# A two-layer decoder step on one core: the decay/alpha low-rank layer run on raw rows, token-shift differences on GpSimd

## The reference, cut to what matters

```python
h = _rmsnorm(x, p["norm_mix_g"][i])                  # the third norm of the program
h_prev = jnp.concatenate([shift0[:, None, :], h[:, :-1]], axis=1)
xx = h_prev - h
mixed = h[None] + xx[None] * mu[:, None, None, :]
r, k, v = jnp.einsum("sbtd,sde->sbte", mixed[:3], w_rkv)
xv, xw, xa, xg = mixed[2], mixed[3], mixed[4], mixed[5]
w_log = -jax.nn.softplus(-(w0 + jnp.tanh(xw @ w1) @ w2)) - 0.5
alpha = jax.nn.sigmoid(a0 + (xa @ a1) @ a2)
g = jax.nn.sigmoid(xg @ g1) @ g2
```

## Time and profile before

| | before |
|---|---|
| runs, us | 1533.9 (1532.29 to 1537.23) |
| the profiled execution, us | 1532.43 |
| its span, first to last instruction | 1530.0 |
| mean granted TensorE clock | 0.993 |
| busy share PE / DVE / ACT / POOL | 97% / 71% / 56% / 9% |

### The profile page before, as it was taken

The page is one execution under the profiler, slowest core; times in us unless marked ns, Lnnn a source line. Parts: engine busy times, 40 slices in busy tenths (PEclk is TensorE's granted clock), DMA queues, the critical chain, the costliest instruction groups (busy, mean ns, idle before and its releaser), DMA issues.

```text
span 1530.0 us, 26537 instructions
## 1 busy us (share of the span) xinstructions
PE 1489.8 (97%) x11503; PEld 1215.8 (79%) x11503; DVE 1085.8 (71%) x1038; ACT 857.6 (56%) x838; POOL 134.5 (9%) x170
## 2 busy tenths in 40 slices
PE   7999999999999988999999999999999999999997
PEld 7998999999889778986667677776777777777674
DVE  4687455554468664222498898888888888888897
ACT  5444444433364423233367777777777777777775
POOL 0066100000100030133001000000000000000020
PEclk9999999999999999999999999999999999999999
DMA  8643575545345020055599999999999999999992
GB/s 250 191 145 83 150 230 164 164 129 153 83 141 188 4 58 4 21 125 175 204 317 383 382 380 366 383 374 381 386 373 384 364 388 372 366 387 367 381 388 97
DMA packets 250269, 378.05 MB, mean 247 GB/s; under 512 B 28169, under 2 KB 142073, under 8 KB 249858
## 3 DMA queue, kind: packets, MB, share of 16 engines
q1 hardware_dynamic: 247874, 370.04, 69.6%
q0 software_dynamic: 2064, 6.18, 1.2%
q10 hardware_dynamic: 208, 0.07, 0.0%
HBM read 368.47 MB, written 7.78 MB: 246 GB/s over the span
## 4 chain that ended last, share of the span: by engine, by line
PE 94%; DVE 3%; issue 1%; ACT 1%; DMA 0%; ACTq 0%; DVEq 0%
PE bank L2562 46%; PE bank L1927 27%; PE bank L2050 3%; PE bank L2224 1%; PE bank L2209 1%; DVE wL L1612 1%; PE bank L2470 1%; PE bank L2495 1%; PE bank L2571 1%; PE bank L1980 1%; PE bank L2409 1%; PE bank L2543 0%; PE bank L2417 0%; PE bank L2271 0%; DMA vecrows<-b_w 0%
## 5 line engine op out<-in xcount | busy, mean ns | idle before, releaser
L1612 DVE TENSOR_TENSOR wL<-ering,wH 128x2048 fp32r<-128x2048 f32 x264 | 603.4, 2289 | 89.4 <-ACT wH L1105 88.0
L1105 ACT ACTIVATE wH<-ering 128x2048 fp32r<-128x2048 f32 x264 | 506.0, 1917 | 147.5 <-PE bank L2562 147.3
L2562 PE MATMUL bank<-wH,xgH 128*96 128x512 f32 (+1 forms) x768 | 290.1, 378 | 2.0 <-DVE wL L1612 1.6
L2562 PE MATMUL bank<-wH,xgL 128*96 128x512 f32 (+1 forms) x768 | 287.6, 374 | 0.0
L2562 PE MATMUL bank<-wL,xgH 128*96 128x512 f32 (+1 forms) x768 | 287.3, 374 | 0.0
L2562 PEld LDWEIGHTS bank<-wH,xgH 128*96 128x96 f32 x768 | 124.4, 162 | 46.1 <-issue 2.1
L2562 PEld LDWEIGHTS bank<-wH,xgL 128*96 128x96 f32 x768 | 124.3, 162 | 44.3 <-issue 0.3
L2562 PEld LDWEIGHTS bank<-wL,xgH 128*96 128x96 f32 x768 | 124.5, 162 | 42.1
L2562 PE MATMUL bank<-wH,hH 128*96 128x512 f32 x352 | 139.5, 396 | 0.5 <-DVE wL L1612 0.5
L2562 PE MATMUL bank<-wH,hL 128*96 128x512 f32 x352 | 138.3, 393 | 0.0
L2562 PE MATMUL bank<-wL,hH 128*96 128x512 f32 x352 | 137.8, 392 | 0.0
(11 more groups left out here) (432 smaller groups left out, 2548.7 us busy)
## 6 DMA issues: line engine op xcount, KB each, us to landing
ering<-m_w_gate SPq DMA_DIRECT2D x88, 1024.0 KB, 8.2
ering<-m_w_up SPq DMA_DIRECT2D x88, 1024.0 KB, 8.7
ering<-m_w_down SPq DMA_DIRECT2D x88, 1024.0 KB, 7.7
arena<-a_w_in SPq DMA_DIRECT2D x16, 1024.0 KB, 5.8
arena<-b_w_rkv SPq DMA_DIRECT2D x12, 1024.0 KB, 5.2
fring<-f_w_gate SPq DMA_DIRECT2D x11, 1024.0 KB, 5.2
fring<-f_w_up SPq DMA_DIRECT2D x11, 1024.0 KB, 5.2
fring<-f_w_down SPq DMA_DIRECT2D x16, 704.0 KB, 4.7
```

The lines of the kernel that those rows point to most:

```text
L1105: s_.activation(wH[:, hslot(g), :], ering[:, eslot(g), :], ACT.Copy).then_inc(S["e_hi"], 1)
L1612: v.tensor_tensor(wL[:, hslot(g), :], ering[:, eslot(g), :], wH[:, hslot(g), :].bitcast(F32), ALU.subtract).then_inc(S["e_lo"], 1)
L2562: mm = t.matmul(dst, lhs[l], rhs[r], start=(start and m == 0), stop=(stop and m == 2), skip_group_check=True)
```

## The change

- The product of `wa` with the rows no longer uses the normalised `hT`. GpSimd first multiplies `wa` by the norm gain (`wa_g`), TensorE multiplies `wa_g` by the raw rows `xT` into bank 0, in the middle of the sum of squares, and VectorE applies the factor `rinv` to the result (`rt`). The product of `wa_mu` with `xxT` goes to bank 1 of its own, and VectorE adds it to `rt`. ScalarE then reads `rt` instead of bank 0.
- The prompt differences move from VectorE (one instruction, eight chunks) to GpSimd (three instructions, for chunks 0-1, 2-4 and 5-7), each started when its normalised chunks are there. The gate mix and the `wa_mu` matmuls wait per group.
- The low part of the first key weights moves from VectorE to GpSimd, behind the differences.
- The key mix and its low parts alternate on VectorE, chunk by chunk, two chunks apart.
- The transposes of the last rows move behind the `wa_mu` product, and ScalarE's copies of them behind the high part of the first key weights.
- SyncE issues pieces 65 and 66 ahead of the stores of the last rows.
- The semaphore `masks` is renamed `pool_out`, with new counts; this is left out below.

```diff
...
         WA = 62
         wa = slot(WA % RING, "p (k n) -> p k n", n=DC * P, k=DC)
         wa_mu = view(B[8], DC * P, "p (k n) -> p k n", k=DC)
+        wa_g = view(B[8] + DC * P, DC * P, "p (k n) -> p k n", k=DC)
+        GROUPS = ((0, 2), (2, 5), (5, 8))
...
-stream(24, 65)
+stream(24, 67)
 sp.wait_ge(S["end_rows"], 2)
 sp.dma_start(out["shift_prompt"].rearrange("a b d -> (a b) d"), shrow[0:1, :]).then_inc(S["shift_out"], 16)
 sp.dma_start(out["shift_sample"].rearrange("a b d -> (a b) d"), shrow[1:1 + NB, :]).then_inc(S["shift_out"], 16)
-stream(65, len(pieces) - 5)
+stream(67, len(pieces) - 5)
...
-norm_add(2, tokens(B[7]))
 pool.wait_ge(landed[WA % RING], arrival[WA])
 mu_wa = vec[:, col["b_mu"] + 24:col["b_mu"] + 40].rearrange("p (i k) -> p k i", i=2)
 pool.wait_ge(S["ffu_ready"], FC)
+gain_wa = vec[:, col["norm_mix_g"] + 8:col["norm_mix_g"] + 16]
+g.tensor_tensor(wa_g, wa, bc(gain_wa, 2, [P, DC, P]), ALU.mult).then_inc(S["pool_out"], 1)
+norm_add(2, tokens(B[7]))
 g.tensor_tensor(wa_mu.rearrange("p k (i n) -> p k i n", i=2), wa.rearrange("p k (i n) -> p k i n", i=2),
-                bc(mu_wa, 3, [P, DC, 2, LW]), ALU.mult).then_inc(S["masks"], 1)
+                bc(mu_wa, 3, [P, DC, 2, LW]), ALU.mult).then_inc(S["pool_out"], 1)
+for lo, hi in GROUPS:
+    pool.wait_ge(S["h_ready"], DC + hi)
+    g.tensor_tensor(xxT[:, lo:hi, 1:NP_], hT[:, lo:hi, 0:NP_ - 1], hT[:, lo:hi, 1:NP_], ALU.subtract) \
+        .then_inc(S["pool_out"], 1)
+pool.wait_ge(S["f_hi"], KV_HI + 1)
+g.tensor_tensor(lowW[KV % RING][:, :], slot(KV % RING, None), kvW[0][:, :].bitcast(F32), ALU.subtract) \
+    .then_inc(S["f_lo"], 1)
 pool.wait_ge(S["shift_out"], 32)
...
 norm_act(2, tokens(B[7]))
 s_ = nc.scalar
 s_.preload_act_table_set("sigmoid_and_others")
-for hf in range(2):
-    act.wait_ge(S["end_tr"], hf + 1)
-    s_.activation(shrow[:, 512 * hf:512 * hf + 512], banks[4 + hf][0:1 + NB, :], ACT.Copy) \
-        .then_inc(S["end_rows"], 1)
 def kv_w_high(j):
     act.wait_ge(landed[(KV + j) % RING], arrival[KV + j])
     if j >= 3:
...
         s_.activation((xkH, xvH)[m][:, c, :], (m1T, m0T)[m][:, c, :], ACT.Copy).then_inc(S["f_xh"], 1)
 
 kv_w_high(0)
-act.wait_ge(S["masks"], 1)
-act.wait_ge(S["lo1_ready"], 1)
-s_.activation(lw1, banks[0][0:LW, 0:T], ACT.Tanh).then_inc(S["lo1_done"], 1)
-s_.activation(la1, banks[0][LW:P, 0:T], ACT.Copy).then_inc(S["lo1_done"], 1)
+for hf in range(2):
+    act.wait_ge(S["end_tr"], hf + 1)
+    s_.activation(shrow[:, 512 * hf:512 * hf + 512], banks[4 + hf][0:1 + NB, :], ACT.Copy) \
+        .then_inc(S["end_rows"], 1)
+act.wait_ge(S["pool_out"], 1)
+act.wait_ge(S["xx_ready"], 7)
+s_.activation(lw1, rt[0:LW, :], ACT.Tanh).then_inc(S["lo1_done"], 1)
+s_.activation(la1, rt[LW:P, :], ACT.Copy).then_inc(S["lo1_done"], 1)
 kv_x_high(0)
-act.wait_ge(S["lo1_ready"], 2)
+act.wait_ge(S["lo1_ready"], 3)
...
 v.tensor_copy(lastc[:, :, 0:1], hT[:, :, NP_ - 1:NP_]).then_inc(S["xx_ready"], 1)
 v.tensor_copy(lastc[:, :, 1:1 + NB], hs[:, :, :, NS - 1]).then_inc(S["xx_ready"], 1)
 
-v.tensor_tensor(xxT[:, :, 1:NP_], hT[:, :, 0:NP_ - 1], hT[:, :, 1:NP_], ALU.subtract).then_inc(S["xx_ready"], 1)
 v.tensor_scalar(xxT[:, :, 0:1], hT[:, :, 0:1], -1.0, None, ALU.mult).then_inc(S["xx_ready"], 1)
 v.tensor_tensor(xs[:, :, :, 1:NS], hs[:, :, :, 0:NS - 1], hs[:, :, :, 1:NS], ALU.subtract) \
     .then_inc(S["xx_ready"], 1)
 shift = vec[:, col["state_shift"]:col["state_shift"] + 64].rearrange("p (b c) -> p c b", c=DC)
 v.tensor_tensor(xs[:, :, :, 0], shift, hs[:, :, :, 0], ALU.subtract).then_inc(S["xx_ready"], 1)
-dve.wait_ge(S["xx_ready"], 6)
-
-def mix(n, i):
-    for c in range(DC):
+dve.wait_ge(S["lo1_ready"], 1)
+v.tensor_tensor(rt[:, :], banks[0][:, 0:T], rinv[:, :], ALU.mult).then_inc(S["xx_ready"], 1)
+dve.wait_ge(S["xx_ready"], 5)
+
+def mix(n, i, lo=0, hi=DC):
+    for c in range(lo, hi):
         v.scalar_tensor_tensor(out=mixbuf[n % 2][:, c, :], in0=xxT[:, c, :], scalar=vcol("b_mu", 8 * i + c),
                                in1=hT[:, c, :], op0=ALU.mult, op1=ALU.add).then_inc(S["mx_ready"], 1)
 
...
     v.tensor_tensor(lowW[(KV + j) % RING][:, :], slot((KV + j) % RING, None), kvW[j % 3][:, :].bitcast(F32),
                     ALU.subtract).then_inc(S["f_lo"], 1)
 
-def kv_x_low(m):
+def kv_x_low(m, lo=0, hi=DC):
     raw, high, low = ((m1T, xkH, xkL), (m0T, xvH, xvL))[m]
-    for c in range(DC):
+    for c in range(lo, hi):
         dve.wait_ge(S["f_xh"], KV_XH + DC * m + c + 1)
         v.tensor_tensor(low[:, c, :], raw[:, c, :], high[:, c, :].bitcast(F32), ALU.subtract) \
             .then_inc(S["f_xl"], 1)
 
-mix(0, 5)
-mix(1, 1)
-kv_w_low(0)
-kv_x_low(0)
+for n, (lo, hi) in enumerate(GROUPS):
+    dve.wait_ge(S["pool_out"], 4 + n)
+    mix(0, 5, lo, hi)
 dve.wait_ge(S["lo1_ready"], 2)
+dve.wait_ge(S["xx_ready"], 6)
+v.tensor_tensor(rt[:, :], banks[1][:, 0:T], rt[:, :], ALU.add).then_inc(S["xx_ready"], 1)
+for c in range(DC + 2):
+    if c < DC:
+        mix(1, 1, c, c + 1)
+    if c >= 2:
+        kv_x_low(0, c - 2, c - 1)
+dve.wait_ge(S["lo1_ready"], 3)
 mix(2, 2)
+dve.wait_ge(S["f_lo"], KV_HI + 1)
 kv_w_low(1)
 kv_x_low(1)
...
-norm_pe(2, tokens(B[7]))
-
 n_piece[0] += 1
 assert n_piece[0] == WA + 1
-pe.wait_ge(landed[WA % RING], arrival[WA])
-pe.wait_ge(S["xt_ready"], 3 * DC)
+sq2 = tokens(B[7])
+pe.wait_ge(S["sq_sum"], 2 * (DC - 2))
+t.matmul(banks[6][:, 0:T], ones[:, :], sq2[:, 0, :], start=True, stop=False, skip_group_check=True)
+pe.wait_ge(S["pool_out"], 2)
+pe.wait_ge(S["xt_ready"], 2 * DC + 5)
 for k in range(DC):
-    pe.wait_ge(S["h_ready"], DC + k + 1)
-    t.matmul(banks[0][:, 0:T], wa[:, k, :], hT[:, k, :], start=(k == 0), stop=False)
-pe.wait_ge(S["xx_ready"], 2)
-for hf in range(2):
-    for j in range(4):
-        mm = t.transpose(banks[4 + hf][0:1 + NB, P * j:P * j + P], lastc[:, 4 * hf + j, :], ident[:, :])
-    mm.then_inc(S["end_tr"], 1)
+    if k == 2:
+        pe.wait_ge(S["sq_ready"], 2 * DC)
+        t.matmul(banks[6][:, 0:T], ones[:, :], sq2[:, DC - 1, :], start=False, stop=True, skip_group_check=True) \
+            .then_inc(S["norm_sum"], 1)
+        pe.wait_ge(S["xt_ready"], 3 * DC)
+    mm = t.matmul(banks[0][:, 0:T], wa_g[:, k, :], xT[:, k, :], start=(k == 0), stop=(k == DC - 1),
+                  skip_group_check=True)
+mm.then_inc(S["lo1_ready"], 1)
 
 def project(bank, w, x, ks, inc, first_wait=None):
     for k in range(ks):
...
     if inc:
         mm.then_inc(S[inc], 1)
 
-pe.wait_ge(S["xx_ready"], 6)
-pe.wait_ge(S["masks"], 2)
-for k in range(DC):
-    mm = t.matmul(banks[0][:, 0:T], wa_mu[:, k, :], xxT[:, k, :], start=False, stop=(k == DC - 1))
+pe.wait_ge(S["xx_ready"], 5)
+for n, (lo, hi) in enumerate(GROUPS):
+    pe.wait_ge(S["pool_out"], 4 + n)
+    for k in range(lo, hi):
+        mm = t.matmul(banks[1][:, 0:T], wa_mu[:, k, :], xxT[:, k, :], start=(k == 0), stop=(k == DC - 1))
 mm.then_inc(S["lo1_ready"], 1)
+for hf in range(2):
+    for j in range(4):
+        mm = t.transpose(banks[4 + hf][0:1 + NB, P * j:P * j + P], lastc[:, 4 * hf + j, :], ident[:, :])
+    mm.then_inc(S["end_tr"], 1)
```

More of the change, by code:

```diff
@@ L289, in trunk_kernel @@
             v_tr v_evac v_aggr std_ready v_rstd v_norm mix_ready mix_done ao_ready ffg_ready ffu_ready
-            sg_ready hf_ready fd_ready masks end_tr end_rows shift_out xx_ready mx_ready
+            sg_ready hf_ready fd_ready pool_out end_tr end_rows shift_out xx_ready mx_ready
             lo1_ready lo1_done lo2_ready lo2_done kvr_ready kvr_done kk_raw kk_sq kn_ready kn_root kk_chain
@@ L332, in trunk_kernel @@
                (lambda s: slot(s, "p (k n) -> p k n", n=DC * P, k=DC)[:, :, LW:P], a["b_a1"][0].rearrange("(k p) n -> p k n", p=P))],
-              "lo1_ready", 1)
+              "pool_out", 3)
         piece([(lambda s: slot(s, "p (k n) -> p k n", n=DC * LG, k=DC), a["b_g1"][0].rearrange("(k p) n -> p k n", p=P))],
-              "lo1_ready", 2)
+              "lo1_ready", 3)
         piece([(lambda s: slot(s, None, parts=LW, n=D), a["b_w2"][0]),
@@ L721, in _ @@
             step(g.memset(segm[:, 0:NP_].rearrange("p (n s) -> p n s", s=CH)[:, :, 0:1], 0.0))
-            g.memset(segm[:, NP_:T].rearrange("p (n s) -> p n s", s=NS)[:, :, 0:1], 0.0).then_inc(S["masks"], 1)
+            g.memset(segm[:, NP_:T].rearrange("p (n s) -> p n s", s=NS)[:, :, 0:1], 0.0).then_inc(S["pool_out"], 1)
             norm_add(1, tokens(B[2]))
-            norm_add(2, tokens(B[7]))
             pool.wait_ge(landed[WA % RING], arrival[WA])
@@ L733, in _ @@
             pool.wait_ge(S["rb_ready"], DC)
-            g.tensor_copy(XT, bc(id64, 1, [P, 2 * H, 64]).rearrange("p (i h) t -> p i h t", i=2)).then_inc(S["masks"], 1)
-            pool.wait_ge(S["masks"], 3)
-            g.tensor_copy(XTq[SB], bc(id64[SB, SMP:2 * SMP], 1, [SMP, H, SMP])).then_inc(S["masks"], 1)
+            g.tensor_copy(XT, bc(id64, 1, [P, 2 * H, 64]).rearrange("p (i h) t -> p i h t", i=2)).then_inc(S["pool_out"], 1)
+            pool.wait_ge(S["pool_out"], 7)
```

(7 more changed lines are left out.)

## The result

| | before | after |
|---|---|---|
| runs on one chip, us (9 each) | 1534.52 (1531.96 to 1540.23) | 1545.62 (1542.9 to 1562.56) |
| ratio after / before | | 1.0089, 95% interval 1.0064 to 1.0114 |
| the profiled execution, us | 1532.43 | 1561.4 |
| its span | 1530.0 | 1559.0 |
| mean granted TensorE clock | 0.993 | 0.977 |

The change makes the kernel slower by 9.8 to 17.5 us (0.64% and 1.14% of 1534.5). The forecast was 1541.9 with a range up to 1544.5: right in sign, 3.7 us low in the median, and the median lies 1.1 us outside the range. Ratios and medians compare fast executions alone: of the kernel before's 35 in the later set with the delay and the kernel after again, two (1554.68 and 1555.44 us) ran in a slower state and are left out.

The account below looks back on a forecast made before the run. TensorE was taken to bound the kernel. Keys at 430.25 + 13.80 + 1.7 = 445.75 instead of 437.72, +8.0 us on the profiled 1532.4, gave 1540.4; the median, 1.5 above, 1541.9. Range 1532.5 to 1544.5.

Parts of the forecast that it names:

- what bounds: Whole kernel: TensorE, busy 97% of the span and 94% of the chain; only what stops or slows it counts.
- the yardstick: From `wa_mu` product to keys: keys start at S + 13.80 us plus the clock's cost; break-even S is 423.92.
- the clock term: From `wa_mu` product to keys: 1.7 us lost to TensorE's lower clock after idling, between 0 and 3.9.
- the lock: Norm and differences: GpSimd and VectorE go first come, first served, one instruction at a time, released 0.14 us before the end.
- who is blocked: Around the third norm: VectorE's norm, sample differences and mixes, all reading two SBUF tiles; the state difference stands 4.4 us.
- the first rival: Before the `wa_mu` product: the last small difference slips in ahead of the key low part; +3.8 us, 1537.7; chance 0.22.
- the state difference short: Last small VectorE difference before the `wa_mu` product: near 4.5 us long if the prediction is right, short if wrong.
- the norm and GpSimd's prices: Third norm: 6.3 us instead of 3.5; GpSimd's difference groups 1.3, 1.8 and 1.8 us, key low part 4.4.
- 1.5 to 2.1: Sign of being right: GpSimd's three prompt differences behind the norm take 1.5 to 2.1 us.
- two of them at 1.3 us or more: Sign of being right: of the eight norm instructions on VectorE, two take 1.3 us or more.
- off the path, at nothing: Raw `wa_g` product around the second sum of squares: its 8 matmuls fill TensorE's idle stretch and cost nothing.
- every microsecond by which the keys start earlier or later goes through to the end: From the keys on: the chain stays on TensorE to the next stage, so the keys' +8.0 us reaches the end.

Follow-up runs that it names:

- the delay: The kernel before with the prompt differences computed three times more on VectorE, ahead of the ones that count; 1547.35 us, ratio 1.0081.
- the added add: The kernel before plus one GpSimd add of 2016 columns reading two SBUF tiles, started behind the second norm chunk; 1538.67 us, ratio 1.0018.
- the memset: The kernel before plus one GpSimd memset of 2016 columns into unused memory, started behind the second norm chunk; 1536.43 us, ratio 1.0000.
- both on VectorE: The kernel after with the prompt differences and the low part of the first key weights back on VectorE; 1539.84 us, ratio 1.0015.
- the pause filled: The kernel after with differences and key low part back on VectorE, plus nine unused matmuls behind the raw product; 1540.79 us, ratio 1.0002.

## Why the prediction was right and where it was wrong

**Right: what bounds, and the yardstick.** The keys start at S, the start of the `wa_mu` product, + 13.80 plus the clock. After, the parts behind the product take 0.87, 7.88 and 1.17, to the hundredth those of before, and the keys start at 427.66 + 13.80 + 2.66 = 444.12. After's second sum of squares begins 1.8 us earlier than before's (413.83 against 415.64), so S = 427.66 is 429.5 in the frame of the prediction, which had 430.25; the keys are 445.9 where it had 445.75. That they agree so closely is partly luck: S was 0.8 too late and the clock term 1.0 too small (both below), and the two cancel.

**Right: the lock.** First come, first served, a whole instruction, released 0.13 to 0.19 us before the end (for the added add: it ends at 421.87, and the instruction it held ends at 422.19, its own 0.51 taken off 421.68). Rows 9 to 11 said so for other lines, and after shows it on four pairs, the add on a fifth that was made for it. The Trainium skill, "SBUF — State Buffer", section "Who interferes with whom", is borne out in both directions: a VectorE instruction with two SBUF inputs is held by a GpSimd instruction that reads SBUF (4.69 against 0.51) and not by one that only writes it (the norm at 3.52 beside the memset).

**Right with a wrong detail: who is blocked.** I had listed norm, sample differences and mixes, the instructions with two SBUF inputs, and let the copies and the first column pass. What stood behind the third group was a copy (1.49 for 0.21), and what stood behind the low part was the first column, a multiply by a constant with one input (4.49 for 0.17). The same section of the Trainium skill's page "SBUF — State Buffer" says that `copy` and `tensor_scalar` can be held as well, in a mode that uses both read ports; I had read the rule narrowly, and the trace bears it out by these two rows. With it the first rival falls away: there is no race of 0.1 us between the last small difference and the low part, because three small VectorE instructions stand behind it, one of them at the door. I gave that rival 0.22 on a margin that did not exist. The sum was not changed by it, since the block lasts as long whichever instruction is the one. But one of the prediction's own signs of being wrong came true by it, "the state difference short": it took 0.26.

**Slightly off: the norm and GpSimd's prices.** The norm takes 5.5, not 6.3: the groups take 1.24, 1.67 and 1.46 instead of 1.3, 1.8 and 1.8, and only two of them fall into the norm. The third met the copy. The low part takes 4.49 for 4.4. Together S came 0.8 earlier than computed. Of the signs, GpSimd's three at "1.5 to 2.1" and "two of them at 1.3 us or more" (1.29 and 1.71) were met in part.

**Mis-sized: the clock.** The term was 1.7, taken from the one comparable row, with 0 to 3.9 as bounds. After has 2.7, and 2.3 to 3.3 in the other profiles with such a pause (products of 6.14 to 7.18, the last in after, again). Those of before are two short idle stretches with matmuls between them; after has one of 10.2 us, in the waits of after (who waited for whom, us, times, longest):

```profile
PE bank L2080 <- DVE arena L1432: 10.2, 1, 10.2
```

This is also what the raw product cost. I had booked it as off the path, at nothing. It is off the path, but it had been the cover that kept TensorE busy: with it gone from there, 2.4 us came back in the product behind (6.25 for 3.88 with both on VectorE; the passage is 26.09, and 24.00 with the pause filled). The product's start was only 0.7 us earlier for it.

**Wrong: that the keys' delay goes through to the end and nothing is added behind it, and so the range.** This is the step that failed: "every microsecond by which the keys start earlier or later goes through to the end", with all that lies behind the keys put at nothing. The passage came out within 0.2 us of the forecast, but the median was missed by 3.7: 0.6 is the kernel before, whose median was 1534.52 in this comparison against the 1533.9 from which I had started; 0.2 is the passage; 2.9 lie outside it. Of what lies outside, 1.8 us are the lower clock (0.91 for 1.00) in the first 20 us of the delta-rule stage, which all ten profiles with another passage than before's show; the cause of the rest stays open, and it is within what executions of one kernel differ by. The range carried the bounds of the terms in the passage and no term for what the rest of the program does. In later sets the kernel before lies between 1530.55 and 1541.38 (29 executions) and between 1531.53 and 1548.6 (35), while the passages of its two profiles are 0.3 apart. Three runs within 5 us of each other had made that look small. With 2 us more at the top for it, the range would have reached 1546.5 and held the time.

## What to carry to other kernels

Before moving an instruction that reads SBUF to GpSimd, write down which VectorE instruction will start next beside it. In this passage each one that did, with one SBUF input or two, stood until GpSimd's was all but done, even if it was eight columns wide; and where TensorE waits for it, the price is nearly GpSimd's full length. Where the move is kept, let GpSimd wait until the small instructions on the path are through; that one wait was worth 3.8 us here. And matmuls that are "only" filling a pause hold the clock up: taking them out earlier gives back in the next product what was gained.

## What the runs showed of the hardware that I had not expected

- A copy of 8 columns and a multiply of 8 columns, each 0.17 us alone, took 4.35 and 4.49 beside a GpSimd instruction. Width does not protect, one input does not either.
- A GpSimd memset of 2016 columns takes 1.78 us and lengthens none of VectorE's instructions that read two tiles, while an add of the same size takes 4.64 and holds one of them.
- GpSimd gets its turn between VectorE instructions that follow one another: the add started 0.16 us behind a norm instruction that still ran, and the next one stood. Nothing like the 6.47 us of the earlier trace rows appeared in the passage; at its old place, near 97 us, it is in every run (6.44 to 6.48), and it stays unexplained.
- The same instructions in the delta-rule stage, about 4017 matmuls, took from 177.9 to 196.9 us, at mean granted clocks from 0.99 to 0.90, in kernels that leave the stage untouched; among two executions of the kernel after alone, 180.1 and 196.9. Its first 20 us, which begin 75 us behind the passage, ran at a granted clock of 1.00 in the three profiles with the passage of before and at 0.91 in the ten others, whose passages are from 1.2 us shorter to 8.9 us longer.
